# The idle matrix products in norms, scans and preparation taken out of a two-block transformer kernel on one core

## The reference

```python
def first_block(x, c, ...):                  # two layers
    h = x * (1 + sc_m) + sh_m                # scale and shift from c
    mix = token_mixers(h, ...)               # attention over the top 128 keys, retention, mLSTM
    x = layer_norm(ALPHA * x + (1 + g_m) * mix, ln_mix_g, ln_mix_b)
    h = x * (1 + sc_f) + sh_f
    x = layer_norm(ALPHA * x + (1 + g_f) * moe_ffn(h, ...), ln_ffn_g, ln_ffn_b)

def head_norm(x):                            # on the outputs of retention and mLSTM
    return (x - mean(x)) * rsqrt(var(x) + LN_EPS)

def second_block(x, p, ...):
    # layer 0: RWKV-7 group and gated delta rule, side by side
    y_a = rwkv7_group(...)                   # decays, l2norm(k * k_k), scan, group norm, gate
    y_b = gdn_group(...)                     # l2norm of q and k, chunked delta rule, rmsnorm
    x = x + concatenate([y_a, y_b]) @ even_w_out
    # layer 1: banded attention; both layers: MLP and a gated embedding
```

## Time and profile before

| | us |
|---|---|
| median of three runs | 3422.65 (3420.23 to 3423.28) |
| the profiled execution | 3424.4 |
| its span, first to last instruction | 3422.6 |
| mean granted TensorE clock over the span | 0.937 |

### The profile page before, as it was taken

How to read it: one execution, slowest core, us unless ns; L and a number is a source line. 1 busy time by engine, 2 the same in 40 slices (tenths; PEclk the granted TensorE clock), 3 DMA queues, 4 the chain that set the end, 5 groups by cost and what they waited for, 6 DMA issues and landing times. The chain is left out here.

```text
span 3422.6 us, 47005 instructions
## 1 busy us (share of the span) xinstructions
PE 3122.9 (91%) x18896; PEld 2531.4 (74%) x18896; DVE 2254.1 (66%) x3391; ACT 1324.7 (39%) x1883; POOL 751.0 (22%) x679
## 2 busy tenths in 40 slices
PE   8987888999998698999898698889999998999999
PEld 7873677887884577787774586777888887777887
DVE  6888757996887765898664775554533695754424
ACT  2234534774332633776321222132222435622322
POOL 0227511001135621000530341211000255410000
PEclk9997888999997788999999898999999998999999
DMA  7850004994542000898121000012222222222222
GB/s 284 265 170 4 1 19 166 376 375 178 195 159 70 1 22 38 334 376 322 41 95 68 2 4 2 2 68 86 91 95 98 99 87 69 68 94 86 95 92 84
DMA packets 62280, 408.78 MB, mean 119 GB/s; under 512 B 7664, under 2 KB 9328, under 8 KB 14960
## 3 DMA queue, kind: packets, MB, share of 16 engines
q1 hardware_dynamic: 56304, 363.84, 29.5%
q0 software_dynamic: 5760, 41.95, 3.5%
HBM read 396.31 MB, written 2.10 MB: 116 GB/s over the span
## 5 line engine op out<-in xcount | busy, mean ns | idle before, releaser
L146 PE MATMUL ps<-t_part,weight_hi 128*128 128x512 f32 x2024 | 801.6, 396 | 17.5 <-DVE scr_part L519 13.3
L148 PE MATMUL ps<-t_part,ring_lo 128*128 128x512 f32 x2024 | 792.0, 391 | 0.0
L471 ACT CAST weight_hi<-ring 128x2048 fp32r<-128x2048 f32 x140 | 267.8, 1913 | 734.1 <-PE ps L148 734.1
L147 PE MATMUL ps<-scr_part,weight_hi 128*128 128x512 f32 x1384 | 543.2, 392 | 0.0
L481 DVE TENSOR_TENSOR ring_lo<-ring,weight_hi 128x2048 fp32r<-128x2048 f32 x140 | 334.7, 2391 | 280.1 <-ACT weight_hi L471 280.1
L146 PEld LDWEIGHTS ps<-t_part,weight_hi 128*128 128x128 f32 x2024 | 383.0, 189 | 100.8 <-issue 14.9
L148 PEld LDWEIGHTS ps<-t_part,ring_lo 128*128 128x128 f32 x2024 | 382.7, 189 | 80.7
L147 PEld LDWEIGHTS ps<-scr_part,weight_hi 128*128 128x128 f32 x1384 | 263.1, 190 | 57.2 <-issue 3.3
L147 PE MATMUL ps<-big_part,weight_hi 128*128 128x512 f32 x768 | 299.7, 390 | 0.0
L147 PEld LDWEIGHTS ps<-big_part,weight_hi 128*128 128x128 f32 x768 | 144.7, 188 | 30.2
L190 POOL TENSOR_TENSOR big<-big 128x512 f32<-128x512 f32 x28 | 53.0, 1891 | 448.9 <-ACT big L183 446.7
(11 more groups left out here) (692 smaller groups left out, 7016.7 us busy)
## 6 DMA issues: line engine op xcount, KB each, us to landing
ring<-in_w_moe SPq DMA_DIRECT2D x84, 1024.0 KB, 5.0
t<-in_w_moe SPq DMA_DIRECT2D x84, 1024.0 KB, 5.0
ring<-in_w SPq DMA_DIRECT2D x64, 1024.0 KB, 4.9
t<-in_w_ada POOLq DMA_DIRECT2D x40, 1024.0 KB, 5.5
ring<-in_w_in SPq DMA_DIRECT2D x32, 1024.0 KB, 6.8
ring<-in_even_in SPq DMA_DIRECT2D x15, 1024.0 KB, 4.9
ring<-in_qkv SPq DMA_DIRECT2D x12, 1024.0 KB, 4.9
ring<-in_w_out SPq DMA_DIRECT2D x8, 1024.0 KB, 4.8
```

Source lines behind the costliest of these rows:

```text
L146: pe.matmul(bank, w_hi, x_hi, start=first, stop=False)
L147: pe.matmul(bank, w_hi, x_lo, start=False, stop=False)
L148: return pe.matmul(bank, w_lo, x_hi, start=False, stop=last)
L471: s.copy(K.w_hi[:, g % 2, :], K.ring[:, g % NSLOT, :]).then_inc(self.w_hi.up(), 1)
```

## The change

The loop in `keep_busy` runs over nothing, so all its 34 products are gone. Waits ahead of the calls stay (L2833 still waits in `rwkv_decays`), and nothing else is touched.

```diff
 def keep_busy(K, pe, count, bank=7):
 
-    for _ in range(count):
+    for _ in range(0):
         pe.matmul(K.ps[:, bank, :], K.mean_d[:, :], K.tri[:, 2:6, :], start=True, stop=True)
```

## The result

| | before | after |
|---|---|---|
| median of the runs of one measurement, us | 3424.12 (3420.23 to 3427.28, 6 runs) | 3438.53 (3433.42 to 3445.16, 6 runs) |
| the profiled execution, us | 3424.4 | 3445.16 |
| mean granted clock over the span | 0.937 | 0.924 |

The ratio is 1.0044, with a 95% interval of 1.0032 to 1.0056: 15 us slower, 11 to 19. The forecast had the sign, and the time lies in its range near the upper end. The size was about half: +7.8 predicted. The time is above the 3426 to 3436 that the prediction gave to its own case, and beside the 3439 of a rival.

What follows compares the result with a forecast made beforehand. It took the path to run in turns over PE, DVE and ACT, the clock low where PE had little to do. Terms -4.0 + 3.4 + 4.5 + 2.0 + 1.9 = +7.8 us gave 3430.4, range 3418 to 3440.

Steps and rivals of the forecast that it cites:

- its own case: Whole kernel: all five terms hold as worked out, 3426 to 3436 us; chance 0.52.
- the rival in which the clock falls in the layer norms: Layer norms also run partly at the low clock and the scan's end costs its upper price: +16.5 us, 3439; chance 0.12.
- Terms 1 and 2: Ends of mlstm: next stage starts sooner, -4.0 us; head norms behind them begin at the low clock, +3.4 us.
- term 2: Head norms behind mlstm: they begin at the low clock and their mean products run slower, +3.4 us.
- Term 3: Spreads in the norms: without the single products ahead of them the clock falls sooner, inside the spreads, +4.5 us.
- Term 4: rwkv_decays: without its eight products the clock stays low into rwkv_opening, +2.0 us.
- Term 5: Ends of the RWKV scans: the clock falls sooner after the first and may fall after the second, +1.9 us.
- Nothing, for rwkv_mix and the layer norms: rwkv_mix and the layer norms: taking their idle products out changes nothing, 0 us.
- The clock does as before: Falls stay behind the spreads and head norms are quick; only the mlstm saving is left, -4.0 us, 3418.7; chance 0.10.
- PE's time comes back: 29 us of idle records were in somebody's way; at most 3 us more comes off, 3416; chance 0.03.
- About even: rwkv_decays price holds, falls move less than spreads need, second scan's end stays full: +2.4 us, 3425; chance 0.23.

Runs made afterwards that it cites:

- a1: Only the six idle products at the ends of mlstm taken out of the kernel before: 3425.57 us, ratio 1.0007.
- c1: The kernel before, unchanged, traced a second time: 3421.36 us, mean clock 0.935.
- a2: Only the eight idle products in rwkv_decays taken out of the kernel before: 3429.31 us, ratio 1.0017.
- a3: Only the six idle products of feature_norm, one in each, taken out of the kernel before: 3429.41 us, ratio 1.0015.
- a4: Only the four idle products at the ends of the RWKV scans taken out of the kernel before: 3429.22 us, ratio 1.0012.
- b1: Only the idle products in rwkv_mix (six) and the four layer norms (one each) taken out of the kernel before: 3424.59 us, ratio 0.9995.
- c4: Kernel before with all idle products, DVE computing its first four rwkv_mix tiles twice, shifting what follows by 2.07 us: 3425.36 us, ratio 1.0005.
- b3: Idle products in mlstm, rwkv_mix and the layer norms taken out of the kernel before, the rest kept: 3426.66 us, ratio 1.0009.
- b4: As b3, with idle products added behind each spread, ahead of NormAhead's spread and at starts of projections: 3432.53 us, ratio 1.0018 to the kernel before.
- c2: The changed kernel, all idle products out, traced a second time: 3438.82 us, mean clock 0.926.
- b2: All 34 idle products of the kernel before kept, with operands of 4 rows instead of 128: 3446.54 us, ratio 1.0059.

## Why the prediction was right in sign and short in size

**Terms 1 and 2, mlstm's ends and head norms: -0.6 predicted, +1.5 in the traces, +2.4 (-1.0 to +5.5) timed alone (a1).** The mechanism of each was right: the start moved forward by 2.0 us, and DVE's first reading came 0.96 later. The step that failed is "behind six records that took 4.42 us", taken as what these records cost in every execution. In c1 they take 3.31, and then the saving is 0.9 a layer while term 2's price stays. With the idle products, the four sections are 14.67, 14.52, 13.64 and 13.65, without them 14.44, 14.43, 15.39 and 15.28. The traces of the other runs make this miss smaller than these eight values do: of ten more sections with the products (a2, a3, a4, b1, c4) nine have 14.6 to 14.8 and one 13.65, and all six of a1, b3 and b4, which lack those of `mlstm` and keep those of `feature_norm`, have 14.43. Over all of them the two ends of `mlstm` come to about nothing, 28.9 us with and 28.9 without, for the -0.6 predicted.

**Term 3, the spreads: +4.5 predicted, 6.05 in the traces (1.25 + 1.27 + 1.35 + 2.18), +5.1 (1.7 to 8.2) timed alone (a3).** Right in mechanism for kk and the group norm, a size too small: the fall is earlier in a spread than the 1.1 us that I took, or at its start (a3: 8.13 for 4.75). The kk spread took 7.25 to 7.28 us in c2, a3 and b2, 4.75 in the changed kernel's first trace, and never over 4.88 in the ten traces with its full product. The fall is also not the same in every execution, 14.2 and 11.5 us for q and k in two traces of the same kernel, and 11.3 to 12.4 in ten with the product in. The output norm's 2.18 is in both traces of the changed kernel. But a3, without that norm's idle product, has 4.87, and b2, with a thin one, as well, so it isn't the work of its own idle product; what moved the fall there isn't shown.

**Term 4, rwkv_decays: +2.0 predicted, +2.0 in the opening, +1.4 more in the inverse; +5.8 (2.7 to 8.9) timed alone (a2).** The term that I trusted most was right for the stage it was worked out for (its 1.86 us to a group stands in no row; with the 1.98 of the earlier trace rows it would be +1.9), and the sum was still short, since it stopped at the end of that stage. Behind it the clock is low again at the inverse, where groups of 32 stand on the path, for 6.8 us instead of 3.4 or none. a2 has both without any other edit. Of its +5.8 some 2.4 are in no section that I can assign: its trace has 1.6 us more in the second inverse and scan, which b3 has in part (0.6) with the eight kept. The interval reaches down to 2.7.

**Term 5, the scans' ends: +1.9 predicted; in the traces +1.0 in the group norm up to L993, +1.1 in the second inverse and scan; timed alone +4.1 (1.0 to 7.5).** The case that no row showed came in: it falls in the group norm. a4 has its scan unchanged, 57.80 us, so the 0.8 us of it in the changed kernel isn't shown to come from these four. Only the +1.0 is.

**Nothing, for rwkv_mix and the layer norms:** b1 bears it out, and with it the rival in which the clock falls in the layer norms goes: 3439 was nearly the time measured, by another way. *The clock does as before* fell with the windows, *PE's time comes back* with a1. *About even* rested on a full clock at the scan's end and falls that barely moved; both went the other way. So the range was met at the edge that this rival had opened, and with a sum of half the size: that the time fell into it was partly luck.

**The sum.** Found at the terms' places in the two pairs of traces: 1.5 + 6.05 + 3.4 + 2.1 = 13.1, against 7.8. The missing 5.3 are 2.1 in terms 1 and 2, 1.6 in term 3, 1.4 in term 4 and 0.2 in term 5; the shares of terms 1 and 2 and of the spread of q and k are within what traces of one kernel differ by. Up to the measured 15, 2 us are left, in projections and the first block, where a stretch at the low level starts or ends a little elsewhere. What they hang on isn't settled.

**The low time.** The mean clock gives the low share, twice one minus the clock: 12.6% of 3422.6 us and 15.2% of 3443.3, 431 and 523 us; in c1 and c2 445 and 509. So the changed kernel has 64 to 92 us more at the low level; some 14 and 24 of them lie ahead of the first place that was changed, and the 50 and 68 us behind it go with 15 to 16 us more time. The Trainium skill (TensorE: Matmul & The Clock Gate, Part 1) prices a low stretch at half its length here, which would be 25 to 34, an estimate by that rule. The runs don't agree: in `rwkv_decays` 3.72 of 30.70 low microseconds are PE's at all, and in the norms its turns lie between waits for DVE and ACT.

## What to carry to other kernels

Price an idle product by what the clock does in the next two or three stages, not by whether it ends last in its own: here eight products that stood on nobody's path kept the opening quick, and mostly the inverse behind it. It pays where PE waits for others and short products on the path follow (34 of them are worth 15 us in 3424, by the single runs nearly all by 18); between dense products or before a long idle stretch it did nothing here (b1), and added ahead of dense work it brought no gain (b4). Don't read what such a product costs or saves out of one trace: two traces of one kernel differed by up to 2.7 us in a section, and two traces of each kernel still gave +1.5 for terms 1 and 2 where more gave nothing.

## What the runs showed of the hardware that I had not expected

- Products of four rows didn't raise the clock in the 14.02 us of sixteen records in a row; with 128 rows the same records raise it within 9.87 us (b2).
- The same kernel rises and falls at other places in each execution. Up to the first changed instruction, traces of kernels that are the same up to there differ by up to 8 us (the last L1729 of the first layer starts at 416.84 in b4, at 424.55 in the changed one), and 34 runs of the kernel before reach from 3416.26 to 3431.44. The Trainium skill (TensorE: Matmul & The Clock Gate, Part 1) says that the number of slow products at a kernel's start varies from run to run of one kernel; further into the kernel the traces show the same, with 4.42 and 3.31 us for the same six records.
- Whether the clock falls again soon after a rise isn't set by the products just ahead alone. In the changed kernel it came back at 1945.5, was low again at 1952.3, and stayed so for 6.8 us; in the kernel before it rose at 1926.9, and the next low stretch began at 1940.5 and took 3.4. In c1, the same kernel, it rose at 1923.9 and stayed full through the whole scan. It isn't just that the changed kernel's rise is later: a3, with the eight products in, has the earliest rise of all, counted from the first L2805, and a low stretch of 6.8 us at the inverse all the same. What decides it isn't shown.

```profile
1923.90:2009.30 85.40, 73.31 (x2063) 65.22 (x2061) 58.06 (x129) 18.14 (x38) 31.93 (x35) 1.00 0.01 3
```
